# The first expert's rows after a mixture-of-experts loop: scaled and added by VectorE instead of GpSimd

## The reference, cut to what matters

```python
f = rmsnorm(h, ffn_norm_g[i])
h = h + moe_swiglu(f, router_w[j], moe_w1[j], moe_w3[j], moe_w2[j])   # 2 of 8 experts a token
gate = jax.nn.sigmoid(rmsnorm(h, ple_norm_g[i]) @ ple_gate_w[i])
h = h + gate * (p[i] @ ple_proj_w[i])
```

## Time and profile before

| | |
|---|---|
| median of 3 runs | 1831.36 us (1830.05 to 1832.8) |
| the profiled execution | 1830.01 us |
| its span in the profile | 1828.2 us |
| mean granted PE clock | 0.981 |
| PE busy | 1754.7 us (96%) |
| DVE busy | 1362.0 us (74%) |
| ACT busy | 1221.8 us (67%) |
| POOL busy | 45.4 us (2%), 33 instructions |
| DMA | 510 MB, mean 279 GB/s |

### The profile page before, as it was taken

The page is one execution under the profiler, slowest core; times in us unless marked ns, Lnnn a source line. Parts: engine busy times, 40 slices in busy tenths (PEclk is TensorE's granted clock), DMA queues, the critical chain, the costliest instruction groups (busy, mean ns, idle before and its releaser), DMA issues.

```text
span 1828.2 us, 26305 instructions
## 1 busy us (share of the span) xinstructions
PE 1754.7 (96%) x9303; PEld 1497.1 (82%) x9303; DVE 1362.0 (74%) x1591; ACT 1221.8 (67%) x1533; POOL 45.4 (2%) x33
## 2 busy tenths in 40 slices
PE   8999988999999989999999999999999999999985
PEld 7877767989998868988888888888888888888864
DVE  4466756656666455669989989899898998998963
ACT  5545654565444355668787787887878878778763
POOL 0000000000000000010000000000000000000041
PEclk9999998999999999999999999999999999999997
DMA  9843233427955444339999999999999999999971
GB/s 333 266 168 101 90 116 111 166 99 288 379 185 207 138 164 158 139 144 370 372 378 394 365 397 374 375 391 362 389 383 377 392 370 373 395 363 401 371 267 46
DMA packets 76688, 510.07 MB, mean 279 GB/s; under 512 B 8282, under 2 KB 8410, under 8 KB 19280
## 3 DMA queue, kind: packets, MB, share of 16 engines
q1 hardware_dynamic: 70240, 484.17, 69.0%
q0 software_dynamic: 6384, 25.01, 4.4%
HBM read 484.51 MB, written 24.64 MB: 278 GB/s over the span
## 4 chain that ended last, share of the span: by engine, by line
PE 87%; DVE 5%; ACT 3%; issue 2%; POOL 1%; DMA 1%; POOLq 0%; SPq 0%; DVEq 0%; ACTq 0%
PE ps L1664 22%; PE ps L1665 22%; PE ps L1669 22%; PE ps L1918 4%; PE ps L1925 4%; PE ps L1919 4%; PE ps L1647 3%; DVE wlo L1049 2%; DVE sg L1178 1%; POOL y_low L613 1%; ACT sg L816 1%; PE ps L2022 1%; PE ps L1740 1%; ACT whi L658 1%; ACT xh L674 0%
## 5 line engine op out<-in xcount | busy, mean ns | idle before, releaser
L1049 DVE TENSOR_TENSOR wlo<-raw,whi 128x1024 fp32r<-128x1024 f32 x906 | 1047.7, 1217 | 179.2 <-ACT whi L658 176.1
L658 ACT ACTIVATE whi<-raw 128x1024 fp32r<-128x1024 f32 x906 | 905.5, 1057 | 129.0 <-PE ps L1669 107.3
L1664 PE MATMUL ps<-whi,xgh 128*128 128x512 f32 x896 | 353.5, 394 | 0.8 <-DVE xgl L1613 0.8
L1665 PE MATMUL ps<-whi,xgl 128*128 128x512 f32 x896 | 348.9, 389 | 0.0
L1669 PE MATMUL ps<-wlo,xgh 128*128 128x512 f32 x896 | 276.4, 390 | 0.0
L1664 PE MATMUL ps<-whi,xh 128*128 128x512 f32 (+1 forms) x432 | 177.7, 413 | 22.1 <-issue 10.0
L1669 PEld LDWEIGHTS ps<-wlo,xgh 128*128 128x128 f32 x896 | 168.2, 188 | 35.5
L1664 PEld LDWEIGHTS ps<-whi,xgh 128*128 128x128 f32 x896 | 168.3, 188 | 34.5 <-issue 1.0
L1665 PEld LDWEIGHTS ps<-whi,xgl 128*128 128x128 f32 x896 | 168.4, 188 | 33.5
L1664 PE MATMUL ps<-whi,mTh 128*128 128x512 f32 x448 | 175.9, 393 | 0.0
L1665 PE MATMUL ps<-whi,mTl 128*128 128x512 f32 x448 | 174.4, 389 | 0.0
(11 more groups left out here) (321 smaller groups left out, 1762.8 us busy)
## 6 DMA issues: line engine op xcount, KB each, us to landing
raw<-in_w_moe_dram SPq DMA_DIRECT2D x336, 1024.0 KB, 7.3
raw<-in_w_fixed_dram SPq DMA_DIRECT2D x112, 1024.0 KB, 5.1
tokens_scratch<-zeros POOLq DMA_DIRECT2D x1, 8704.0 KB, 44.3
y_scratch<-zeros POOLq DMA_DIRECT2D x2, 2304.0 KB, 55.3
y_scratch<-yo SPq DMA_DIRECT2D x18, 256.0 KB, 7.7
xin<-tokens_scratch SPq DMA_DIRECT2D x8, 512.0 KB, 8.0
bias_scratch<-revb POOLq DMA_DIRECT2D x1, 3072.0 KB, 38.8
bias<-bias_scratch POOLq DMA_DIRECT2D x1, 2048.0 KB, 17.4
```

Source lines behind the costliest of these rows:

```text
L658: AC(whi[:, v % SPL, c], raw[:, v % RAW, c], ACT.Copy).then_inc(high_done, 1)
L1049: V.tensor_tensor(wlo[:, v % SPL, c], raw[:, v % RAW, c], whi[:, v % SPL, c].bitcast(F32), ALU.subtract).then_inc(low_done, 1)
L1664: mm(o, hi(k0 + k, T), wh[:, k, :], start=first and k == 0, stop=False)
L1665: mm(o, lo(k0 + k, T), wh[:, k, :], start=False, stop=False)
```

## The change

Four edits.

1. POOL no longer multiplies and adds. It issues the low gathers in the order of column halves (half 0 of both `T`, then half 1), each half with a semaphore of its own, and goes straight on to wait for the last stores and gather the `y_last` rows.
2. DVE does for the low rows what it does for the last: `add_rows(0, half)` waits for `low_fetched[half]` and does `h += gk * y_low`, 2 instructions a half. The order in DVE's program is low half 0, low half 1, last half 0, transposed remainder, last half 1. Each low pair is followed by a wait of DVE for its own completion (`step`).
3. In every round of the loop ACT copies column half 0 of the result to `yo` before the second half of the round's last split instead of after it. The copy waits only for the store of its own half of the round before (`rows_stored[0]`), no longer for both.
4. Three semaphores (`low_scaled`, `low_added`, the single `low_fetched`) go, two come.

The core of the diff:

```diff
             pool.wait_ge(low_rows_stored, 1)
-            for T in range(NT):
-                for half in range(2):
-                    fetch(0, T, half, y_low, low_fetched)
-            pool.wait_ge(low_fetched, 64)
-            for T in range(NT):
-                ins = pool.tensor_scalar(y_low[:, T, :], y_low[:, T, :], gk[:, 0, T:T + 1], None, ALU.mult)
-            ins.then_inc(low_scaled, 1)
-            pool.wait_ge(low_scaled, 1)
-            pool.tensor_tensor(h[:], h[:], y_low[:], ALU.add).then_inc(low_added, 1)
+            for half in range(2):
+                for T in range(NT):
+                    fetch(0, T, half, y_low, low_fetched[half])
             for half in range(2):
                 pool.wait_ge(last_stored[half], 16)
                 for T in range(NT):
...
-            def split_to(u):
+            def split_to(u, then=None):
...
                         c = slice(half * n // 2, (half + 1) * n // 2)
+                        if then and half and v == u:
+                            then()
                         AC(whi[:, v % SPL, c], raw[:, v % RAW, c], ACT.Copy).then_inc(high_done, 1)
...
-                split_to(ub + UNITS_ROUND - 1 + AHEAD)
+
+                def copy_result(half):
+                    act.wait_ge(rows_stored[half], g.at(rows_stored[half], 16))
+                    act.wait_ge(half_used, g.at(half_used, 2 * (U["ffn1"] + UNITS_ROUND - 1 + half)))
+                    AC(yo[:, half * NB:(half + 1) * NB], ps[:, 4 + half, :], ACT.Copy).then_inc(y_copied, 1)
+
+                split_to(ub + UNITS_ROUND - 1 + AHEAD, lambda: copy_result(0))
+                copy_result(1)
...
-            def add_last(half):
+            def add_rows(k, half):
 
                 c = slice(half * NB, (half + 1) * NB)
-                dve.wait_ge(y_fetched[half], 32)
+                rows, fetched = ((y_low, low_fetched), (y_last, y_fetched))[k]
+                dve.wait_ge(fetched[half], 32)
                 for T in range(NT):
-                    ins = V.scalar_tensor_tensor(out=h[:, T, c], in0=y_last[:, T, c], scalar=gk[:, 1, T:T + 1],
+                    ins = V.scalar_tensor_tensor(out=h[:, T, c], in0=rows[:, T, c], scalar=gk[:, k, T:T + 1],
                                                  in1=h[:, T, c], op0=ALU.mult, op1=ALU.add)
-                ins.then_inc(h_combined, 1)
+                if k:
+                    ins.then_inc(h_combined, 1)
+                else:
+                    step(ins)
...
                 split_to(ub + 2)
-                dve.wait_ge(low_added, 1)
-                add_last(0)
+                add_rows(0, 0)
+                add_rows(0, 1)
+                add_rows(1, 0)
                 turned_low(6, 0)
-                add_last(1)
+                add_rows(1, 1)
```

More of the change, by code:

```diff
@@ L320, in build @@
         low_rows_stored = sem("low_rows_stored")
-        low_fetched = sem("low_fetched")
-        low_scaled = sem("low_scaled")
-        low_added = sem("low_added")
+        low_fetched = [sem(f"low_fetched{half}") for half in range(2)]
         y_fetched = [sem(f"y_fetched{half}") for half in range(2)]
@@ L1015, in _ @@
                 expert(lambda: split_gathered(1))
[L1016 to L1021, removed]
                 assert g.split == U["ffn1"] + UNITS_ROUND + 2
```

## The result

| | before | with the change |
|---|---|---|
| median of 4 runs each | 1832.08 us (1830.05 to 1835.74) | 1821.28 us (1819.2 to 1823.07) |
| ratio to before | | 0.9941, 95% interval 0.9929 to 0.9953 |
| the profiled execution | 1830.01 us, span 1828.2 | 1821.46 us, span 1819.6 |

The change makes the kernel faster by 10.8 us (1832.08 x 0.0059); by the interval of the ratio it is between 8.6 and 13.0 us. I had forecast 12.8 us and 1817.2 us, with a range up to 1821.2; the median lies just outside.

The account below looks back on a forecast made before the run. POOL's serial stretch behind the expert loop was taken as the bound: DVE finishes column half 0 of `h` at 1779.65 instead of 1792.48, gaining 12.8 us from 1830.01 to 1817.2 us; range 1812.8 to 1821.2.

Parts of the forecast that it names:

- What bounds the kernel, and what the change frees: Behind the expert loop: POOL's serial scaling (5.68 us) and adding (4.53 us) delay the last-row gathers; later work moves as one piece.
- The start of the second last-row gather: On POOL behind the loop: first last-row gather at 1769.0, the second, completing half 0, 1.27 us later at 1770.3.
- the four low gathers start at the same times: On POOL: low gathers only change order, so low half 1 still lands at 1775.57 and its adds stay hidden.
- The landing: Second last-row gather takes 7.83 us to land, at 1778.1, like the fourth low gather; the other bound was 3.55 us.
- My upper bound: Last-row gathers squeezed in behind the weights at 442 GB/s land at 1779.5; DVE ends at 1781, gain 11.5 us.
- Three limits that I had named for being right: First last-row gather starts by 1769.5, PE's wait behind the filler is 4.5 to 7 us, landing not after 1780.
- The base: The sum starts from the profiled execution, 1830.01 us, 1.35 us under the median of the runs.
- The VectorE rival: DVE's work on two SBUF operands keeps POOL from issuing the last-row gathers; gain 10.7, 1819.3 us; chance 0.12.
- The stall rival: Last-row gathers on full DMA engines stall 12.2 us: 1829.4 us for one stall, 1841.6 for two; chance 0.04.
- The clock: PE's clock still falls in the shorter wait; the rival that it stays up gave 1814.1 us, chance 0.08.
- Half-wise low semaphores hidden, low half 0 hidden: On DVE: both low pairs of adds finish before the last rows land, low half 1 at 1777.1; cost nothing.
- Edit 3 costs nothing: In the loop: ACT's swap delays the split half 0.58 us, hidden, cost 0; 8 x 0.58 = 4.6 us if uncovered.

Follow-up runs that it names:

- e9_move_only: Against the kernel before: only the move of the adds from POOL to VectorE, low gathers and ACT's copy in the old order; 1824.60 us, ratio 0.9949.
- c_after_again: The changed kernel as it is, measured once more; 1823.10 us, ratio 0.9949 to before.
- e4: The changed kernel with low gathers in the old order on one semaphore, DVE adding after all four; 1820.58 us, ratio 0.9946 to before.
- e1: The changed kernel with the loads of the last two weight units issued before the last round's stores; 1817.11 us, ratio 0.9921 to before.
- e6: The changed kernel with the last two weight units loaded only once the last rows of half 0 have landed; 1815.64 us, ratio 0.9911 to before.
- e2: The changed kernel with one DVE wait a round, making a gap in its run of wlo instructions; 1819.19 us, ratio 0.9931 to before.
- e5: The changed kernel with 38 instead of 6 filler products on PE before the transposes and 12 behind; 1818.80 us, ratio 0.9927 to before.
- e3: The changed kernel with edit 3 undone, ACT copying after the round's last split as before; 1820.47 us, ratio 0.9943 to before.

## Why the prediction was right or wrong

**What bounds the kernel, and what the change frees: right.** The serial stretch on POOL was the loss, the loop didn't change (950.1 us), and what follows the first transposes moved forward as one piece: 35.74 us from half 0 of `h` to the end before, 35.97 and 35.68 after. e9_move_only shows that the move alone is the gain.

**The size: 2.1 us of the 12.8 weren't there. The step that failed is the time at which the second last-row gather has landed**, 11.1 us after R in the forecast (1778.1 - 1767.02) and 13.2 measured. With it half 0 of `h` came at 14.7 instead of 1779.65 - 1767.02 = 12.6. By whole times alone this couldn't be said, since 12.8 us lie within the interval of the gain (8.6 to 13.0); it is read from R on. Two parts:

- *The start of the second last-row gather*, 3.28 us after R by my sum, was at 3.93. The third low gather took 1.6 us. What failed here is "the four low gathers start at the same times": edit 3 puts a `wlo` in their way. I had priced that edit in the loop only, and taken credit for an earlier store for which POOL then never waited.
- *The landing*, the larger part: 7.83 taken, 9.26 found (9.86 in c_after_again). The low add that stretched this gather's issue from 0.95 to 1.49 us isn't the reason: in e4, without it, the landing took 9.5 us. I took the row of a gather that had shared the engines with the weights, although the new ones also have the low gathers in front of them. My upper bound (a landing at 1779.5, 12.5 us after R) was too low as well; why the whole traffic took 0.7 us longer than old traffic plus the new megabyte at 442 GB/s, no run shows. e1 (3.50 us) and e6 show the weights' share; e2 (7.5 us) fits the low rows having a share.

Three limits that I had named for being right were passed, each by little: the first last-row gather started 2.60 us after R (2.48 was the limit), PE waited 7.82 us for DVE (7), and the landing, counted from R on the times of before, is at 1780.2 (1780).

**The base.** 1830.01 us was the lowest run of before; its median over 4 runs is 1832.08. With the sum made against one execution, 1.4 us below the median even then, the forecast was too low by that much before any term. Taken from 1832.08 it would have read 1819.3, and the range would have held. This and the landing are of one size, and each is about half of the 4.1 us by which the forecast missed.

**The VectorE rival: the mechanism was right, at another place and price.** I had it hold the two last-row gathers, for 1819.3 us. They lost 0.5 us; what it really holds is the first low gather, for 13 us, and in the changed kernel that is worth 3.2 us (e2). I had the stall in the rows and left it out of what bounds the kernel, since I began the serial stretch at the fourth low gather. My evidence against it, a gather of 0.97 us while DVE was busy, was read too coarsely: that gather started at 1765.18, and the `wlo` of 1764.03 ended at 1765.26 with a gap behind it. The Trainium skill ("SBUF — State Buffer", "Who interferes with whom") says that a VectorE instruction with two SBUF inputs contends with a GpSimd instruction that reads SBUF. The traces agree in this: `wlo` has two SBUF inputs, a gather reads its row numbers (`rowy`), and a gap of 0.13 us ends the stall. They show a hold over more than ten instructions for the first gather and of about one for those behind it.

**The stall rival** (the 13 us belong to gathers on full DMA engines) is out: last-row gathers on full engines took 0.95 to 1.9 us, and the stall follows the gap.

**The clock: right.** It fell in spite of the shorter wait, no gain came with the change, and 2.5 us were there to be had (e5).

**Half-wise low semaphores hidden, low half 0 hidden: right. Edit 3 costs nothing: wrong by 0.7 to 1.0 us (e3).**

## What to carry to other kernels

When serial work is taken out in front of a transfer, the transfer starts in another neighbourhood: price its landing by what is in the queues at the new time, and look which loads that nobody needs yet can step behind it (here 4.6 us of the total, from one wait). Look at an indirect DMA of GpSimd that starts while VectorE runs two-input instructions back to back: here the first one hung for up to 13.8 us, and one small wait on VectorE freed it. Measure such edits from an event beside them: whole times here spread by more than most of the effects.

## What the runs showed that I had not expected

- A gather's stall, 13.2 to 13.8 us without an added gap, ended 0.86 to 0.89 us after VectorE's first moment off, whether that was an added gap of 0.13 us or one of a few hundredths. Later gathers, issued into the same kind of back-to-back run, took 1.93 to 1.97 us and not more. Why they pass between two instructions of the run and the first doesn't stays open.
- Moving one copy of 0.6 us on ACT ahead of a split half made a gather's data land 2.2 us later, through DVE and POOL (e3).
- Unchanged code took between 816.9 and 826.0 us to the same point in 14 profiles. Windows of 5 us up to 815 give 44 us at 1.2 GHz in the profile of 816.9 and 58 us in the two of 826.0. The clock isn't all of it: c_after_again and e2_dve_gap, at 820.7 and 820.9, have 44 us too. What else differs stays open.
